# Gate and up products of a feed-forward layer: one level of block products in 22 units, or two levels in eleven quads

## The chip, the core and the metric

One Trainium2 chip, one core. The metric is device time in microseconds (us) of the whole kernel, median of three runs. A core has a matmul engine (TensorE, PE in the rows; PEld is its weight load), a vector engine (VectorE, DVE), an activation engine (ScalarE, ACT), a general engine (GpSimd, POOL) and SyncE (SP), which here only issues DMA transfers. Each engine works through its own list of instructions in order; between engines, semaphores are waited for.

## The reference, cut to what matters

Two transformer blocks, one after the other, over 1024 tokens of width 1024, all float32. The change is in the feed-forward layer of the first block (D_FF is 2816, three taps):

```python
hn = rms_norm(h, norm_ffn_g[i])
gate = causal_depthwise_conv(hn @ w_ffn_gate[i], ffn_conv_w[i])
h = h + (jax.nn.silu(gate) * (hn @ w_ffn_up[i])) @ w_ffn_down[i]
hn = rms_norm(h, norm_ple_g[i])
h = h + (p[i] @ w_ple_proj[i]) * jax.nn.sigmoid(hn @ w_ple_gate[i])
```

The causal convolution adds, for each hidden channel, the gate value of this token, of the token before and of the one before that, each times its own tap. The second block ends in a squared-ReLU layer of hidden width 4096 (`mlp_w1_2`, `mlp_w2_2`).

## The kernel before

Activations lie with channels on the 128 partitions and tokens along the row. T is 1024 tokens, HALF is 512, P is 128.

**Gate and up, before.** For each of 11 pairs g of 128-channel hidden tiles there are two units, ("gate", g) and ("up", g), each with a 1 MB piece of weights (1024 by 256). A unit is cut into 2 by 2 blocks (input rows, output tiles and token halves) and multiplied with Strassen's seven block products instead of eight. Every product is four matmuls of 128x128 weights on 512 columns (`strassen`, L1936); the trace counts each float32 matmul twice, so a unit is 56 records and all of them 1232. GpSimd makes five weight sums per unit (`sum_of_blocks`, L285), ScalarE copies three products out of PSUM (L2146, L2147, L2151, L2155), VectorE adds the others to them in SBUF (`into`, L2236, one operand in PSUM). After gate, VectorE makes the convolution over all 1024 tokens in three steps per tile (`conv`, L2272 to L2274); ScalarE applies SiLU (L2161); after up, VectorE multiplies (`mul`, L2279); GpSimd makes the four sums T3, T1, T2, T4 of hidden blocks that the down product needs (L2397 to L2402). Seven hidden pieces of 256 KB each are then stored to DRAM (`store_pair`, L2051), three tiles in turn being used for them. The order of the work is written out by hand, unit by unit.

**Quads.** The second block's first MLP product is already made in another way, by the class `Quads`. A quad is 512 output channels of 1024 inputs on 1024 tokens. It is cut into 2 by 2 blocks and multiplied in seven block products by the Winograd form of Strassen, called items (q, m1) and run in the order m1 = 1, 2, 6, 7, 5, 4, 3; each item is cut once more, into seven passes m of two matmuls of 128x128 weights on 256 columns (`product`, L3496), so 14 matmuls or 28 records. Items of quad 0 are plain: 8 matmuls on 512 columns, 16 records (`plain_product`, L3513). Of an item, ScalarE copies passes 1, 5, 6 and 4 (`copy`, names t1, t5, t2, c21, L3533) and VectorE adds pass 2, 3 and 7 to the first three (`add_block`, c11, c12, c22, L3541). TensorE's list mixes two items. In the slot of item n it runs

```python
PASSES = ((1, 0), (7, -1), (5, 0), (2, 0), (4, -1), (6, 0), (3, 0))
```

so passes 7 and 4 of item n - 1 come within item n's slot. Pass 4 of item n waits until VectorE has made c22 of item n. GpSimd makes for each item four weight sums of 256 columns (`level_sums`, L3579 to L3584), at most three items ahead, and for each quad four of 1024 columns, S1 (L3559), S2 (L3563), S3 (L3566) and S4 (L3571). S2 of quad q waits for the last pass of item (q - 1, 3). VectorE puts the items of a quad together with seven additions of 1024 columns (L4731 in the second block, with the four T sums).

**The down product** of both layers is `LastProduct` (L3767), 28 late items over the hidden pieces read back from DRAM. SyncE issues its loads in order behind the last `store_pair`; VectorE makes a weight sum (L3809) and the right-hand sums (L3833 to L3838), GpSimd the left-hand sums (L3790 to L3795).

## Time and profile before

| what | us |
|---|---|
| median of three runs (3221.6 to 3223.73) | 3222.9 |
| span of the profiled execution, first to last instruction | 3218.1 |
| gate and up products, 806.1 to 1341.1 | 535 |
| down product of the first block, 1341.3 to 1588.3 | 247 |
| second block's quads, 2481.9 to 2842.8 | 361 |
| granted TensorE clock, mean of the span | 0.989 |

The profiled execution's own time is listed as its span; what lies around the span is taken from the median, which is 4.8 us above it. TensorE's records are modelled and overlap: a 512-column record reads 0.59 us but the next starts 0.43 us later, so start-to-start distances are what counts. On the other engines the same holds on a small scale.

### The profile page before, as it was taken

The numbers are of one execution on the slowest core, as the hardware profiler recorded it, in microseconds if no ns is written. First come the engines' busy times: TensorE is split into PE (matmuls) and PEld (weight loads), VectorE is DVE, ScalarE is ACT, GpSimd is POOL, SyncE is SP. The second block draws the span as 40 slices with busy tenths as digits, with TensorE's granted clock in tenths as the row PEclk, the third lists the DMA queues.
The fourth block names the chain that finished last, engine by engine and source line by source line (L and its number), as shares of the span: only waits on it lengthen the run. The fifth ranks groups of instructions, "written<-read, shape, count | busy, mean of one in ns | idle before, by whom it ended". The sixth has DMA issues, their size and how long they took to land.

```text
span 3218.1 us, 32376 instructions
## 1 busy us (share of the span) xinstructions
PE 3120.3 (97%) x12306; PEld 1914.3 (59%) x12306; DVE 1809.7 (56%) x2558; ACT 773.7 (24%) x1302; POOL 1101.7 (34%) x855
## 2 busy tenths in 40 slices
PE   8997998999999999999999999999999999999997
PEld 3445564864444444588644554544554588888886
DVE  2386887742544434487634754753124655567877
ACT  3343334321111111000212333413212344410002
POOL 0010020003333333455610100152014698855655
PEclk9999999999999999999999999999999999999998
DMA  4220111241222122475312211102112233366652
GB/s 140 66 66 27 53 31 53 66 158 65 79 98 85 63 98 85 168 260 194 129 53 80 66 53 57 62 33 90 62 53 78 105 138 144 118 232 246 228 191 91
DMA packets 206121, 334.88 MB, mean 104 GB/s; under 512 B 10128, under 2 KB 123280, under 8 KB 205200
## 3 DMA queue, kind: packets, MB, share of 16 engines
q1 hardware_dynamic: 205968, 332.81, 29.8%
q8 instruction: 100, 1.64, 0.2%
q14 instruction: 53, 0.43, 0.0%
HBM read 268.55 MB, written 64.23 MB: 103 GB/s over the span
## 4 chain that ended last, share of the span: by engine, by line
PE 86%; DVE 8%; POOL 3%; ACT 2%; issue 1%; DMA 1%; DVEq 0%; POOLq 0%; SPq 0%; ACTq 0%
PE psum L1936 16%; PE psum L3767 15%; PE psum L181 10%; PE psum L3496 8%; PE psum L2555 8%; PE psum L407 7%; PE psum L1981 3%; PE psum L4334 3%; PE psum L563 1%; DVE arena L1380 1%; DVE arena L1378 1%; PE psum L3513 1%; PE psum L4311 1%; PE psum L4272 1%; PE psum L1987 1%
## 5 line engine op out<-in xcount | busy, mean ns | idle before, releaser
L3767 PE MATMUL psum<-arena 128*128 128x256 f32 x2660 | 579.4, 381 | 7.1 <-POOL arena L3793 7.1
L3767 PEld LDWEIGHTS psum<-arena 128*128 128x128 f32 x2660 | 506.7, 191 | 78.8 <-POOL arena L3793 8.6
L1936 PE MATMUL psum<-arena 128*128 128x512 f32 x1232 | 530.1, 592 | 1.9 <-DVE arena L2314 1.9
L1936 PEld LDWEIGHTS psum<-arena 128*128 128x128 f32 x1232 | 233.7, 190 | 296.6 <-issue 291.5
L407 PE MATMUL psum<-arena 128*128 128x512 f32 x768 | 337.9, 599 | 7.1 <-DVE arena L1236 4.9
L181 PE MATMUL psum<-arena 128*128 128x512 f32 x768 | 332.4, 592 | 1.5 <-ACT arena L4504 1.5
L2236 DVE TENSOR_TENSOR arena<-arena,psum 128x512 f32<-128x512 f32 x176 | 117.0, 686 | 296.3 <-PE psum L1936 154.7
L407 PEld LDWEIGHTS psum<-arena 128*128 128x128 f32 x768 | 146.2, 192 | 189.6 <-issue 185.0
L181 PEld LDWEIGHTS psum<-arena 128*128 128x128 f32 x768 | 145.8, 190 | 182.1 <-issue 180.6
L2555 PE MATMUL psum<-arena 128*128 128x512 f32 x576 | 251.7, 595 | 0.0
L3496 PE MATMUL psum<-arena 128*128 128x256 f32 x1080 | 244.6, 380 | 6.3 <-DVE arena L3541 5.6
L285 POOL TENSOR_TENSOR arena<-arena 128x512 f32<-128x512 f32 x130 | 162.9, 1287 | 187.5 <-DMA arena<-w_ffn_gate 174.6
L3496 PEld LDWEIGHTS psum<-arena 128*128 128x128 f32 x1080 | 204.1, 190 | 38.5 <-DVE arena L3541 6.6
L2555 PEld LDWEIGHTS psum<-arena 128*128 128x128 f32 x576 | 109.1, 191 | 136.6 <-issue 136.6
L4731 DVE TENSOR_TENSOR arena<-arena 128x1024 f32<-128x1024 f32 x88 | 141.0, 1603 | 12.9 <-ACT arena L3524 8.4
L3790 POOL TENSOR_TENSOR arena<-arena 128x512 f32<-128x512 f32 (+1 forms) x49 | 71.5, 1459 | 209.8 <-PE psum L3767 61.8
L4851 POOL TENSOR_TENSOR arena<-arena 128x512 f32<-128x512 f32 x75 | 98.5, 1313 | 102.5 <-DVE arena L4608 71.1
L3376 POOL TENSOR_TENSOR arena<-small_sb,consts_sb 128x512 f32<-128x512 f32 x16 | 16.2, 1041 | 325.4 <-PE psum L2633 170.6
L2365 POOL TENSOR_TENSOR arena<-arena 128x512 f32<-128x512 f32 x42 | 56.4, 1343 | 170.3 <-ACT arena L2120 169.4
L1981 PE MATMUL psum<-arena 128*128 128x512 f32 x256 | 112.5, 592 | 0.0
L4334 PE MATMUL psum<-arena 128*128 128x512 f32 x224 | 97.0, 593 | 0.9 <-DVEq L241 0.9
L2146 ACT ACTIVATE arena<-psum 128x512 f32<-128x512 f32 x22 | 13.1, 597 | 320.3 <-PE psum L1936 320.3
(552 smaller groups left out, 4374.2 us busy)
## 6 DMA issues: line engine op xcount, KB each, us to landing
arena<-w_in SPq DMA_DIRECT2D x42, 1024.0 KB, 5.2
arena<-mlp_w SPq DMA_DIRECT2D x72, 512.0 KB, 7.0
arena<-w_ffn_down SPq DMA_DIRECT2D x36, 512.0 KB, 7.3
arena<-mlp_w SPq DMA_DIRECT2D x8, 2048.0 KB, 8.6
mlp_hidden_T<-arena SPq DMA_DIRECT2D x32, 512.0 KB, 2.6
arena<-mlp_hidden_T SPq DMA_DIRECT2D x16, 1024.0 KB, 5.6
arena<-w_out SPq DMA_DIRECT2D x12, 1024.0 KB, 5.2
mlp_hidden_B<-arena SPq DMA_DIRECT2D x24, 512.0 KB, 2.6
```

What stands on the lines that cost most here:

```text
L181: mm = nc.tensor.matmul(self.out(i, x.shape[1]), part, x, start=(kk == 0), stop=(kk == self.kt - 1))
L285: return g.tensor_tensor(to[:, 0:kn, :], block_of(*a), block_of(*b), op)
L407: mm = nc.tensor.matmul(ps, slot(u)[:, k, m * P:(m + 1) * P], hn(k, h), start=(k == 0), stop=(k == KD - 1))
L1936: mm = nc.tensor.matmul(ps, left, right, start=(k == 0), stop=(k == 3))
L1981: mm = nc.tensor.matmul(ps, raw(v)[:, k, m * P:(m + 1) * P], half_of(env, N0, k, h), start=(k == 0), stop=(k == KD - 1))
L2236: return v_.tensor_tensor(dst, dst, tiles.ps(*key), op)
L2555: mm = nc.tensor.matmul(ps, slot(n)[:, k, m * P:(m + 1) * P], x_half(k, h), start=(k == 0), stop=(k == KD - 1))
L3496: mm = self.env.nc.tensor.matmul(self.ps(n, m), left[:, k, :], right[:, k, :], start=(m in (1, 5, 2) and k == 0), stop=(k == 1), skip_grou ...
L3767: mm = self.env.nc.tensor.matmul(ps[:, 256 * r:256 * r + 256], left[:, s, r * P:(r + 1) * P], right[:, s, :], start=(first and s == 0 and ...
L4334: mm = nc.tensor.matmul(ps, left, mix_right[m](k), start=(k == 0), stop=(k == 3))
L4731: blocks.mark(v_.tensor_tensor(to, one, two, op), name, q)
L4851: fin(pool, nc.gpsimd.tensor_tensor(dst, dst, src, ALU.add), sem, value)
```

## The change

Gate and up of a pair become one quad of 512 output channels: the left two tiles of it are gate, the right two are up. Eleven quads and 77 items take the place of 22 units; quad 0 is plain, ten quads run in two levels. The products' parts are put together by seven additions per quad (`combine`). The convolution is made per token half h: ScalarE makes the tap of this token with one Identity activation for each of the two tiles (`first_tap`), VectorE adds the other two (`conv`); for the second half two more pairs of instructions, of two and of one column, add what comes from the first half, whose last two columns were put aside (`past`). `mul` is per token half. The T sums go from GpSimd to VectorE. There is one hidden buffer instead of three, so the first tap of quad g waits until the pieces of quad g - 1 are stored. GpSimd now makes `level_sums`. Two thirds of the constants' tile is used as buffer meanwhile and read back from DRAM (one DMA of 128x1280 words). The down product's items and products are the same; its buffers lie elsewhere and its first loads are issued in another order. The second block is as before.

```diff
-            for unit in strassen_units[2:]:
-                for m in order_of[unit[0]]:
-                    strassen(unit, m)
+            for n, m in passes(LAST_N, quads.plain):
+                if m in ("p0", "p1"):
+                    quads.plain_product(pe, n, m)
+                else:
+                    quads.product(pe, n, m)
+                if (n, m) == (0, "p0"):
+                    sum_squares(1)
+                elif (n, m) == (0, "p1"):
+                    root_rows(1)
...
+    items = [(0, 1), (0, 2), (1, 1), (1, 2)] + [(0, m1) for m1 in QUAD_ORDER[2:]] + [(1, m1) for m1 in QUAD_ORDER[2:]]
+    items += [(q, m1) for q in PAIRS[2:] for m1 in QUAD_ORDER]
...
+            q, m1 = items[n]
+            added = [(name, q) for name in {6: ("U2", "C11"), 7: ("U3",), 5: ("U4", "C22"), 4: ("C21",), 3: ("C12",)}.get(m1, ())]
+            if q == 1 and m1 in (3, 6, 7, 5):
+                added += {6: ends(0)[1:2], 7: ends(0)[2:4], 5: ends(0)[4:], 3: ends(1)[1:2]}[m1]
+            elif m1 in (3, 4):
+                added += {3: ends(q)[0:1] if q == 0 else ends(q)[1:2], 4: ends(q)[0:1] if q else []}[m1]
+            elif m1 in (1, 2):
+                added += {1: ends(q - 1)[2:4], 2: ends(q - 1)[4:]}[m1]
...
+            def first_tap(g, h):
+                hidden.wait(act, ("C11", "C12")[h], g)
+                if h == 0:
+                    if g:
+                        act.wait_ge(*stored(g - 1))
+                    else:
+                        made_late.wait(act, at_item[0, 3], "p1")
+                        hidden.wait(act, "C12", 0)
+                for r in range(2):
+                    ins = nc.scalar.activation(hid(h)[:, r, :], (a_, c_)[h][g > 0][:, r, :], ACT.Identity, scale=tap(2, 2 * g + r))
+                copy.mark(ins, "tap", g, h)
...
-            def conv(g, j):
-                i, from_, to = 2 * g + j, made["gate"][j], hid(j, g)
-                if g >= 3 and j == 0:
-                    dve.wait_ge(*stored(g - 3))
-                step.step(dve, v_.tensor_scalar(to, from_, tap(2, i), None, ALU.mult))
-                step.step(dve, v_.scalar_tensor_tensor(to[:, 1:T], from_[:, 0:T - 1], tap(1, i), to[:, 1:T], ALU.mult, ALU.add))
-                hidden.mark(v_.scalar_tensor_tensor(to[:, 2:T], from_[:, 0:T - 2], tap(0, i), to[:, 2:T], ALU.mult, ALU.add), "conv", g, j)
+            def conv(g, h):
+                copy.wait(dve, "tap", g, h)
+                to, from_ = hid(h), (a_, c_)[h][g > 0]
+                taps = lambda j: [tap(j, 2 * g + r) for r in range(2)]
+                if h == 0:
+                    v_.tensor_copy(past, from_[:, :, HALF - 2:HALF])
+                base = step.n
+                for r in range(2):
+                    step.mark(v_.scalar_tensor_tensor(to[:, r, 1:], from_[:, r, 0:HALF - 1], taps(1)[r], to[:, r, 1:], ALU.mult, ALU.add))
+                for r in range(2):
+                    dve.wait_ge(tap_done, base + 1 + r)
+                    ins = v_.scalar_tensor_tensor(to[:, r, 2:], from_[:, r, 0:HALF - 2], taps(0)[r], to[:, r, 2:], ALU.mult, ALU.add)
+                if h:
+                    for r in range(2):
+                        step.mark(v_.scalar_tensor_tensor(to[:, r, 0:2], past[:, r, :], taps(0)[r], to[:, r, 0:2], ALU.mult, ALU.add))
+                    for r in range(2):
+                        dve.wait_ge(tap_done, base + 3 + r)
+                        ins = v_.scalar_tensor_tensor(to[:, r, 0:1], past[:, r, 1:2], taps(1)[r], to[:, r, 0:1], ALU.mult, ALU.add)
+                hidden.mark(ins, "conv", g, h)
...
+            def mul(g, h):
+                to = hid(h)
+                copy.wait(dve, "silu", g, h)
+                hidden.mark(v_.tensor_tensor(to, to, (d_, e_)[h][g > 0], ALU.mult), "mul", g, h)
...
+            for n in range(LAST_N + 1):
+                if two_level(n - 1):
+                    quads.add_block(dve, n - 1, "c22")
...
+                for key in added_after(n - 2)[1:]:
+                    add_up(key)
+                if two_level(n):
+                    quads.add_block(dve, n, "c11")
+                    if n == LAST_N - 1:
+                        late.right_sums(dve, 0)
+                    quads.add_block(dve, n, "c12")
+                for key in added_after(n - 1)[:1]:
+                    add_up(key)
...
+            conv(10, 1)
             late.right_sums(dve, 1)
+            for key in ends(10)[2:]:
+                add_up(key)
...
             store_pair(10)
             late.load_hidden(sp, 3, before_late_load)
+            sp.dma_start(env.consts[:, 2 * P:12 * P], dr["consts"][:, 2 * P:12 * P]).then_inc(w_summed, 16)
```

TensorE's list from the end of the mixers' output product on; `-` is before, `+` is the changed kernel. L1936 and L3651 work on 512 columns, L3634 is the quads' `product`; the counts are matmuls, two records each.

```order
-L1936 MATMUL psum<-arena 128x512 x4
 L292 MATMUL psum<-consts_sb,arena 128x1 x4
-L1936 MATMUL psum<-arena 128x512 x4
+L3651 MATMUL psum<-arena 128x512 x4
 L299 MATMUL psum<-consts_sb,arena 128x128 x4
-L1936 MATMUL psum<-arena 128x512 x608
-L3767 MATMUL psum<-arena 128x256 x508
+L3651 MATMUL psum<-arena 128x512 x8
+L3634 MATMUL psum<-arena 128x256 x26
```

616 matmuls on 512 columns become 56 of the plain quad and 980 on 256 columns.

VectorE's list before, from the second convolution tile of a pair to its first `mul`: L2236 is `into`, L2272 to L2274 the convolution, L2279 `mul`.

```order
L2272 TENSOR_SCALAR arena<-arena,cols_sb 128x1024 [waits taken1_0]
L2273 SCALAR_TENSOR_TENSOR arena<-arena,cols_sb 128x1023 [waits tap_done_1]
L2274 SCALAR_TENSOR_TENSOR arena<-arena,cols_sb 128x1022 [waits tap_done_1]
L2236 TENSOR_TENSOR arena<-arena,psum 128x512 [waits made_0,copied_1,taken2_0]
L2236 TENSOR_TENSOR arena<-arena,psum 128x512 [waits made_0,copied_1]
L2236 TENSOR_TENSOR arena<-arena,psum 128x512 [waits made_0]
L2236 TENSOR_TENSOR arena<-arena,psum 128x512
L2236 TENSOR_TENSOR arena<-arena,psum 128x512 [waits taken5_0,made_0]
L2236 TENSOR_TENSOR arena<-arena,psum 128x512
L2236 TENSOR_TENSOR arena<-arena,psum 128x512 [waits taken6_0,made_0]
L2279 TENSOR_TENSOR arena<-arena 128x1024 [waits copied_1,taken7_0]
```

The seven additions between the convolution and `mul` take products out of PSUM that TensorE has banks for; nothing on TensorE waits for `conv` or `mul` themselves.

VectorE's list in the changed kernel at the same place, the slots of items (q, 2) and (q, 6): the second token half's convolution (L2350 to L2359) of quad q - 1, then c11 (`conformer`), c12 (`consts_sb`), `mul` of the first half (L2365) and c22.

```order
L2350 SCALAR_TENSOR_TENSOR arena<-arena,cols_sb 128x511 [waits copied_1]
L2350 SCALAR_TENSOR_TENSOR arena<-arena,cols_sb 128x511
L2353 SCALAR_TENSOR_TENSOR arena<-arena,cols_sb 128x510 [waits tap_done_1] x2
L2356 SCALAR_TENSOR_TENSOR arena<-small_sb,cols_sb,arena 128x2 x2
L2359 SCALAR_TENSOR_TENSOR arena<-small_sb,cols_sb,arena 128x1 [waits tap_done_1] x2
L3679 TENSOR_TENSOR arena<-psum,conformer 128x256 [waits ones_made_0,copied_1,hid_ready_1]
L3679 TENSOR_TENSOR arena<-psum,consts_sb 128x256 [waits ones_made_0,copied_1]
L2365 TENSOR_TENSOR arena<-arena 128x2x512 [waits copied_1]
L3679 TENSOR_TENSOR arena<-psum,conformer 128x256 [waits ones_made_0,copied_1]
```

The convolution and the first `mul` stand ahead of c22, the last row, in one list.

SyncE's list in the changed kernel around the last store of hidden pieces (L2154), the load of late item 3's hidden piece and what follows; before, the row of L2190 is not there.

```order
L2154 DMA ffn_hidden_B<-arena 128x512 [waits hid_ready_1]
L2154 DMA ffn_hidden_B<-arena 128x512 x2
L2154 DMA ffn_hidden_T<-arena 128x512 x4
L3842 DMA arena<-ffn_hidden_B 128x2x512 [waits consts_in_0,mem_in_0,ones_made_0]
L2190 DMA consts_sb<-consts 128x1280
L3842 DMA arena<-ffn_hidden_T 128x2x1024 [waits cols_in_0,mem_in_0,consts_in_0,ones_made_0]
L3861 DMA arena<-w_ffn_down 128x2x512 [waits ones_made_0]
```

The loads of late item 4 still come behind the store, with one DMA more between.

## Rows read from the trace of the kernel before

**Rows 1.** The page: busy time of each engine over the span.
```profile
PE 3120.3 (97%) x12306; PEld 1914.3 (59%) x12306; DVE 1809.7 (56%) x2558; ACT 773.7 (24%) x1302; POOL 1101.7 (34%) x855
```

**Rows 2.** Timeline of TensorE: start, length (us), line, operation, count, [idle before].
```profile
806.09 3.60 PE L1936 MATMUL psum<-arena 128*128 128x512 f32 x8
...
815.57 1.16 PE L299 MATMUL psum<-consts_sb,arena 128*128 128x128 f32 x8 [1.55 <-DVE arena L2217]
```

**Rows 3.** Timeline of TensorE from the last unit to the down product.
```profile
1341.13 52.89 PE L3767 MATMUL psum<-arena 128*128 128x256 f32 x244
1395.30 5.02 PE L3767 MATMUL psum<-arena 128*128 128x256 f32 x22 [1.28 <-POOL arena L3793]
```

**Rows 4.** Chain of waits in order of time: start, length, what.
```profile
758.19 48.07 PE psum L181 x112
...
2481.87 3.43 PE psum L3513 x8
...
2842.77 290.27 PE psum L3767 x1344
```

**Rows 5.** Timeline of ScalarE, copies in the second block's quads: t2, t1, t5, t2.
```profile
2733.95 0.39 ACT L3533 ACTIVATE consts_sb<-psum 128x256 f32<-128x256 f32 x1 [0.48 <-PE psum L3496]
2735.67 0.39 ACT L3533 ACTIVATE conformer<-psum 128x256 f32<-128x256 f32 x1 [1.34 <-PE psum L3496]
2737.40 0.39 ACT L3533 ACTIVATE conformer<-psum 128x256 f32<-128x256 f32 x1 [1.34 <-PE psum L3496]
...
2739.99 0.38 ACT L3533 ACTIVATE small_sb<-psum 128x256 f32<-128x256 f32 x1 [0.48 <-PE psum L3496]
```

**Rows 6.** Groups of VectorE instructions by form: busy, mean ns, idle before.
```profile
L2273 DVE SCALAR_TENSOR_TENSOR arena<-arena,cols_sb 128x1023 f32<-128x1023 f32 x22 | 28.2, 1284 | 0.8
...
L2279 DVE TENSOR_TENSOR arena<-arena 128x1024 f32<-128x1024 f32 x20 | 24.5, 1225 | 0.7
...
L3541 DVE TENSOR_TENSOR arena<-psum,conformer 128x256 f32<-128x256 f32 x86 | 36.1, 420 | 20.4 <-PE psum L3496 19.7
```

**Rows 7.** Timeline of ScalarE: four instructions that scale 512 columns.
```profile
2502.91 2.55 ACT L4504 ACTIVATE arena<-arena,cols_sb 128x512 f32<-128x512 f32 x4
```

**Rows 8.** Timeline of GpSimd in the second block's quads: S2, s4, S3.
```profile
2715.00 2.36 POOL L3563 TENSOR_TENSOR arena<-arena 128x1024 f32<-128x1024 f32 x1 [2.69 <-PE psum L3496]
...
2720.47 0.73 POOL L3584 TENSOR_TENSOR arena<-arena 128x256 f32<-128x256 f32 x1
2721.16 2.36 POOL L3566 TENSOR_TENSOR arena<-arena 128x1024 f32<-128x1024 f32 x1
```

**Rows 9.** Timelines of VectorE and GpSimd: tiny additions beside GpSimd's.
```profile
196.64 1.20 DVE L1378 TENSOR_TENSOR arena<-arena 128x60 f32<-128x60 f32 x1
...
200.35 0.25 DVE L1380 TENSOR_TENSOR arena<-arena 128x87 f32<-128x87 f32 x1
...
195.26 4.96 POOL L1659 TENSOR_TENSOR arena<-arena,consts_sb 128x512 f32<-128x512 f32 x4 [6.09 <-DVE arena L1369]
```

**Rows 10.** The same: a multiply-add beside GpSimd's additions.
```profile
3050.89 3.24 DVE L4772 SCALAR_TENSOR_TENSOR arena<-arena 128x2048 f32<-128x2048 f32 x1
...
3051.95 3.31 POOL L3793 TENSOR_TENSOR arena<-arena 128x512 f32<-128x512 f32 x1
```

**Rows 11.** The same: 512 columns on VectorE against 256 on GpSimd.
```profile
2539.02 1.10 DVE L3596 TENSOR_TENSOR arena<-arena 128x512 f32<-128x512 f32 x1
...
2539.54 1.19 POOL L3580 TENSOR_TENSOR consts_sb<-arena 128x256 f32<-128x256 f32 x1
```

**Rows 12.** Busy us by stretch (PE, PEld, DVE, ACT, POOL), clock, DMA share, GB/s.
```profile
2640.00:2810.00 170.00, 169.97 (x784) 148.40 (x783) 97.15 (x128) 73.28 (x144) 150.35 (x129) 1.00 0.35 130
```

**Rows 13.** Start of the down product: DMAs issued by SyncE, and VectorE.
```profile
1350.15 3.13 SPq L2051 DMA_DIRECT2D ffn_hidden_T<-arena  x4
...
1358.10 2.73 SPq L3723 DMA_DIRECT2D arena<-w_ffn_down  x4
...
1369.52 2.29 DVE L3809 TENSOR_TENSOR arena<-arena 128x2048 f32<-128x2048 f32 x1 [6.72 <-DMA arena<-w_ffn_down]
```

More of the change, by code:

```diff
@@ L1832, in weights_of, with passed @@
             return down[:, q + 5 * c:q + 5 * c + n, j]
+        def passed(eng, m1):
+            made_late.wait(eng, *quads.last_pass(at_item[10, m1]))
         def before_late_bank(pe, at):
-            tiles.wait_free(pe, late_banks[at])
+            b = late_banks[at]
+            if at == 0:
+                tiles.wait_free(pe, b)
+                return
+            n, kind = max((n, m) for n in range(LAST_N - 3, LAST_N) for m in (1, 2, 3) if quads.bank_of(n, m) == b)
+            if kind == 1:
+                copy.wait(pe, "c21", n)
+            else:
+                hidden.wait(pe, {2: "c11", 3: "c12"}[kind], n)
```

605 lines of the change are left out of this document (333 added, 272 removed).

## The prediction, made before the changed kernel was run

> **What bounds the kernel now.** I read the page first: TensorE is busy 97% of the span, the next engine 56% [rows 1]. So the end is set by how many matmul columns there are and by what TensorE waits for; every other engine matters only where TensorE waits for it. The timeline of TensorE comes next. Gate and up run from 806.09 to 1341.13, 535.0 us, without a break but for a few waits in the first microseconds, of which the longest is 1.55 [rows 2, 3]. At the seam to the down product TensorE goes on at once and first waits 1.28 us at 1395.30 [rows 3]. Third, I read the second block's quads, since the changed kernel makes gate and up by the same code: the chain of waits has them from 2481.87 to 2842.77 [rows 4]. Last come the timelines of VectorE and GpSimd, to see how these two hold each other up.
>
> **TensorE's work.** The price of a 512-column record is the distance in a full stretch: 112 records in 48.07 us, 0.4292 each [rows 4]. Before: 1232 x 0.4292 = 528.8 us. The price of a two-level item is the distance of one and the same copy in two items that follow each other: 2739.99 - 2733.95 = 6.04 us [rows 5], which is 28 records of 0.2157. After: the plain quad has 7 x 16 = 112 records on 512 columns, 48.1 us; ten quads have 70 items of 6.04 us, 422.8. Together 470.9, which is 57.9 less. The two statistics matmul groups between the first products are in both. Of the 535.0 us, 528.8 are products and about 1.9 statistics, so 4.3 are waits of the start, which go: the reciprocal behind the 1.55 us wait no longer stands behind an addition on VectorE that needs a product. Term: -62.2.
>
> **Start of the quads.** The second block's quads take 360.9 us [rows 4], where 7 x 16 x 0.4292 + 49 x 6.04 = 344.0 and about 3.5 of statistics leave 13.4 of waits. Here the start has the same chain on GpSimd (three operands' sums, three quad sums and the item sums before the first two-level items of quad 1), but less is waited for at the very beginning, since the operand sums of the first block come before the scaling of the second half ends. On the other side, conv(0, 0) now stands before c22 of the second item of quad 1. I take 9, between 3 and 14.
>
> **One place in each quad.** From here on I count from the start of the slot of item (q, 2), called 0; the next slot, of item (q, 6), starts at 6.04. TensorE wants c22 of item (q, 2) for pass 4, the fifth pass of that next slot, 6.04 + 4 x 0.863 = 9.5. What VectorE must do before it, by its list: the second half's convolution of quad q - 1 (four multiply-adds of 511 or 510 columns, two of two and two of one column), c11, c12, mul of the first half, c22.
> It starts with the first tap on ScalarE. ScalarE copies t1 0.95 into the slot (one pass and 0.09), t5 1.73 later (2737.40 - 2735.67) for 0.39 [rows 5], so the tap starts at about 3.05; two scalings of 512 columns at 2.55 / 4 = 0.64 each, the last ending 0.1 later, give 4.4 [rows 7]. VectorE's convolution starts at 4.45.
> Undisturbed it takes 4 x 0.66 (half of 1.284 and a semaphore), 4 x 0.22 for the small ones (the 0.25 us row is the nearest [rows 9]) = 3.5, to 8.0; c11 and c12 0.34 each, mul 1.23, c22 0.42 [rows 6]: 10.35. TensorE waits 0.9 us.
> But GpSimd works beside it. Its S2 waits for the last pass of the quad before, 1.6 us before our slot, and S3 starts 6.16 later (2721.16 - 2715.00) and takes 2.36 [rows 8], which is 4.5 into the slot: just as the convolution starts. Item sums follow it without a gap. What that does can be seen elsewhere in the trace [rows 9]: beside four GpSimd additions of 1.24 us, a VectorE addition of 60 columns takes 1.20 (so do its neighbours, four in all, one for each of GpSimd's), and one of 87 columns falls back to 0.25 when GpSimd's are over. A multiply-add and an addition hold each other up alike [rows 10]. A pair, 512 columns against 256, takes about 1.15 [rows 11]. c22's kind, with one operand in PSUM, keeps its 420 ns beside GpSimd [rows 6]. With strict turns: first multiply-add to 5.05, S3 and the second to 8.0, two more pairs to 10.3, four small ones each behind an item sum of 0.69 (2721.16 - 2720.47 [rows 8]), to 13.1, c11 and c12 to 13.8, mul to 15.1, c22 to 15.5. TensorE waits 15.5 - 9.5 = 6.0 us.
> The Trainium skill, page "SBUF — State Buffer", section "SBUF: two separate sides", states that VectorE with two SBUF inputs and GpSimd share a port pair as an exclusive lock, held for the whole instruction. By that rule the 6.0 would hold in every quad, and the change would lose; the rows agree, and that case is the second rival.
> I take 5.4: in the second block's quads GpSimd is busy 150.35 of 170 us, 88% [rows 12], so 0.9 + 0.88 x 5.1. The place comes in the slots (q, 2) for q = 2 to 10, nine times: +48.6, with bounds of 8 (0.9 each) and 63 (7 each, S2 or another long sum in the way too). Below 0.9 there is nothing, as no list gets shorter by the wait.
> Costed at nothing: ScalarE's work (28 copies, 4 taps and 2 SiLU in a quad are about 15 us of 42); the wait of the first tap for the stores of the quad before (the T sums end some 24 us into our count, their stores 8 later as before [rows 13], the tap comes at 36); conv of the first half, which falls where GpSimd waits for S2; quad weight loads, 2 MB in 42 us. If the cover of the stores were gone, that would cost a few us per quad.
>
> **Seam to the down product.** VectorE ends quad 10 with conv(10, 0), C12, the tap, conv(10, 1), a right sum, two mul and four T sums: 3 + 1.2 + 1.4 + 3.5 + 0.4 + 2.5 + 2.6 = 14.6 us after TensorE's last pass, and the stores of the T pieces start 1.4 behind the last sum, at 16. Before, they started at 1350.15, 9 us after TensorE's last unit, and the loads behind them at 1358.10 [rows 13], 17 us after. Now these loads come at about 24, and 1 more for the constants' DMA. The weights then landed for the sum at 1369.52 [rows 13], 11.4 later, just in time (1.28 us wait [rows 3]). So late item 3 waits about 1.5, item 4 (needed at 33.7, after 156 records of 0.2157; its sum ready at 25 + 11.4 + 2.3 = 38.7) about 5, and 1.5 more for GpSimd's sums, less the 1.28. I take +7, between 3 and 11. The last c22 adds 0.5.
>
> **Sum.** -62.2 + 9 + 48.6 + 0.5 + 7 = +2.9. The profiled span 3218.1 becomes 3221.0; the median of the runs lies 4.8 above the span, so 3225.8, call it 3226. A measurement of this kernel can tell about 0.2%, 6.4 us, from no change.
>
> **Rivals.** First, the turns rarely meet: GpSimd is done or waits for its ring when the convolution comes, or takes its turns between. For it speaks that GpSimd stands idle 20 of 170 us there [rows 12] and VectorE is busy for 57% only; against it, that S3 falls on the spot. Each place costs 1 to 3.5 us: -62.2 + 7 + 9 x 2.2 + 0.5 + 6 = -29, 3194. It decides from 4.4 us per place down, where the sum passes -6.
> Second, and on the other side, c22 in full turns everywhere: 6.0 to 7 us per place, and a quad costs as much as two units did (42.3 + 6 against 112 x 0.4292 = 48.1), so that only the plain quad and the start are left as gain, and seam and start take them: -62.2 + 12 + 9 x 6.6 + 0.5 + 8 = +18, 3241. It decides from 5.8 us per place up.
> Third, GpSimd or another list becomes the bound over the whole quad, not at one place: VectorE's work on two SBUF operands is 9 x 1.23 + 12 x 0.66 = 19 us in a quad and GpSimd's alone 28 x 0.69 + 4 x 2.4 = 29, together more than the 42.3; a steady wait spread over many items would give 45 to 50 us a quad and anything from 3200 to 3260. For it speaks the 88%; against it, that GpSimd in the second block still waits 2.69 us for TensorE before an S2 [rows 8]. That the change would not do what it says can be excluded from TensorE's list.
>
> **How the numbers follow.** My forecast (each place 4.4 to 5.8) has 0.40, the first rival 0.30, the second 0.20, the third 0.10. Faster by over 0.2%: the first rival, a few hundredths of the third, 0.05 of the forecast's lower end, 0.37. Slower: the second, most of the third, the forecast's upper end, 0.36. Within 0.2%: 0.27. The forecast alone, with the start and the seam, spans 3213 to 3235; the range for 8 in 10 reaches into both rivals, from 3190 (1.8 us per place) to 3246.
>
> **What will show it.** In the timeline of TensorE: 28 records per 6.04 us between the waits, 1960 + 112 records in all, and in each quad one idle stretch of about 5 us before pass 4 in the slot of item (q, 6), put down to VectorE's add_block, L3679. In VectorE's timeline L2350 to L2359 stretched from 0.67 and 0.2 to about 1.15 (one near 3) and 0.7. If these stand at 0.67 and 0.2, the first rival holds. If TensorE's waits are spread over items and name GpSimd's level sums, the third. The prediction is wrong in its main step if the idle stretches name another list: the stores, ScalarE's copies or the loads. At the seam, the first weight sum of the down product should start about 7 us later, counted from TensorE's last quad pass, than it did (28.4).

## The result, and the profile after

| | before | after |
|---|---|---|
| median of the runs, us | 3222.25 (4 runs) | 3280.36 (3277.49 to 3281.84, 4 runs) |
| profiled span, us | 3218.1 | 3278.4 |
| gate and up, from TensorE's first product to its last pass | 535.0 | 583.7 |
| down product, to the next statistics | 247.0 | 254.9 |
| second block's quads | 360.9 | 363.3 |

The ratio is 1.018, with a 95% interval of 1.0165 to 1.0194: 58 us slower, where 3226 us and at most 3246 were forecast. The first line of the page, which answers to [rows 1]: TensorE is busy for less time than before, and the time is longer.

```profile
PE 3098.1 (95%) x13146; PEld 2088.2 (64%) x13146; DVE 2024.9 (62%) x2806; ACT 864.7 (26%) x1552; POOL 1293.7 (39%) x1025
```

Where the time goes shows in one quad of TensorE's timeline (start, length, line, shapes, count, [idle before]; L3634 is the quads' product). The rows left out are passes without a wait.

```profile
1185.16 1.89 PE L3634 MATMUL psum<-arena 128*128 128x256 f32 x8
1188.73 6.31 PE L3634 MATMUL psum<-arena 128*128 128x256 f32 x28 [1.68 <-DVE arena L3679]
1200.11 7.40 PE L3634 MATMUL psum<-arena 128*128 128x256 f32 x20 [5.08 <-DVE arena L3679]
...
1215.51 0.70 PE L3634 MATMUL psum<-arena 128*128 128x256 f32 x2 [0.23 <-DVE arena L3679]
```

Two things to see. Every quad has three waits for VectorE's additions (L3679), not one: 1.68 for c22 of item (q, 1), 5.08 for c22 of (q, 2), 0.23 later on. And the 20 records behind the 5.08 us take 7.40 us, where 20 records behind a wait of 1.70 us, one quad later, take 4.58:

```profile
1241.90 4.58 PE L3634 MATMUL psum<-arena 128*128 128x256 f32 x20 [1.70 <-DVE arena L3679]
```

The busy times by stretch say why (us of PE, PEld, DVE, ACT, POOL, then the granted clock of TensorE, DMA share, GB/s):

```profile
1189.00:1195.00 6.00, 6.00 (x28) 4.96 (x27) 5.26 (x4) 2.19 (x5) 5.84 (x5) 1.00 0.00 0
...
1200.10:1204.00 3.90, 3.89 (x9) 3.17 (x10) 1.43 (x2) 0.45 (x2) 0.00 (x0) 0.50 0.02 4
1204.00:1208.00 4.00, 4.00 (x16) 3.29 (x16) 1.40 (x4) 0.70 (x2) 0.41 (x1) 0.77 0.00 0
1208.00:1215.00 7.00, 7.00 (x34) 6.08 (x32) 6.50 (x7) 1.92 (x5) 6.84 (x6) 1.00 0.44 162
```

Before the wait the clock is 1.00 (2.4 GHz), behind it 0.50 (1.2 GHz) for the first 4 us, and 0.77 on the mean of the next 4. From one 1.68 wait to that of seven quads later are 366.3 us (979.35 to 1345.69), 52.3 a quad; 42.3 is its work.

VectorE's timeline up to that wait, the place the prediction worked out:

```profile
1188.26 0.41 DVE L3679 TENSOR_TENSOR arena<-psum,conformer 128x256 f32<-128x256 f32 x1
1189.74 3.21 DVE L2350 SCALAR_TENSOR_TENSOR arena<-arena,cols_sb 128x511 f32<-128x511 f32 x2 [1.07 <-ACT arena L2253]
1192.87 2.35 DVE L2353 SCALAR_TENSOR_TENSOR arena<-arena,cols_sb 128x510 f32<-128x510 f32 x2
1195.14 1.35 DVE L2356 SCALAR_TENSOR_TENSOR arena<-small_sb,cols_sb,arena 128x2 f32<-128x2 f32 x2
1196.42 1.44 DVE L2359 SCALAR_TENSOR_TENSOR arena<-small_sb,cols_sb,arena 128x1 f32<-128x1 f32 x2
...
1198.44 1.28 DVE L2365 TENSOR_TENSOR arena<-arena 128x1024 f32<-128x1024 f32 x1
1199.65 0.41 DVE L3679 TENSOR_TENSOR arena<-psum,conformer 128x256 f32<-128x256 f32 x1
```

The eight multiply-adds take 8.1 us, and a multiply-add of one or two columns takes 0.7. At the end of the last quad, where GpSimd stands idle, the same two small pairs take 0.34 us each:

```profile
1397.65 0.34 DVE L2356 SCALAR_TENSOR_TENSOR arena<-small_sb,cols_sb,arena 128x2 f32<-128x2 f32 x2
1397.91 0.34 DVE L2359 SCALAR_TENSOR_TENSOR arena<-small_sb,cols_sb,arena 128x1 f32<-128x1 f32 x2
```

The wait that wasn't foreseen, 1.68, begins eight microseconds earlier. Timelines of VectorE and GpSimd there:

```profile
1177.75 2.60 DVE L2389 TENSOR_TENSOR arena<-arena 128x1024 f32<-128x1024 f32 x1
...
1182.00 3.98 DVE L2353 SCALAR_TENSOR_TENSOR arena<-arena,cols_sb 128x510 f32<-128x510 f32 x2
...
1176.91 2.36 POOL L3697 TENSOR_TENSOR arena<-arena 128x1024 f32<-128x1024 f32 x1
1181.95 2.35 POOL L3701 TENSOR_TENSOR arena<-arena 128x1024 f32<-128x1024 f32 x1 [2.69 <-PE psum L3634]
```

GpSimd's S1 (L3697) ends at 1179.27, and VectorE's C21 (L2389), which takes 1.2 us elsewhere, is stretched to 2.60 by it. So the first half's convolution begins 1.4 us into the 2.69 us that GpSimd waits before S2 (L3701). Its first pair of multiply-adds fits into the rest, its second pair meets S2 and takes 3.98. So c22 of (q, 1) is late.

### The profile page after: what moved, and what is told of

Its sections match the earlier page's. It is cut to its first block, busy times and chain, and to the rows that moved or that the text cites. A ratio compares the mean times of both kernels' runs of the same rounds, so it can differ in the third digit from the quotient of the medians.

```text
span 3278.4 us, 35350 instructions
## 1 busy us (share of the span) xinstructions
PE 3098.1 (95%) x13146; PEld 2088.2 (64%) x13146; DVE 2024.9 (62%) x2806; ACT 864.7 (26%) x1552; POOL 1293.7 (39%) x1025
## 3 DMA queue, kind: packets, MB, share of 16 engines
q8 instruction: 108, 1.77, 0.2%
## 4 chain that ended last, share of the span: by engine, by line
PE 78%; DVE 13%; issue 3%; POOL 2%; ACT 2%; DMA 1%; SPq 0%; DVEq 0%; POOLq 0%; ACTq 0%
PE psum L3634 17%; PE psum L3905 15%; PE psum L181 10%; PE psum L2690 8%; PE psum L407 7%; PE psum L2083 3%; PE psum L4472 3%; PE psum L3651 3%; DVE arena L2350 1%; PE psum L563 1%; DVE arena L1380 1%; DVE arena L1378 1%; DVE arena L2389 1%; DVE arena L2353 1%; DVE arena L3679 1%
## 5 line engine op out<-in xcount | busy, mean ns | idle before, releaser
L3634 PE MATMUL psum<-arena 128*128 128x256 f32 x2632 | 621.0, 390 | 81.7 <-DVE arena L3679 76.8
L3634 PEld LDWEIGHTS psum<-arena 128*128 128x128 f32 x2632 | 510.7, 195 | 171.4 <-DVE arena L3679 85.9
L3905 PE MATMUL psum<-arena 128*128 128x256 f32 x2660 | 582.4, 382 | 11.5 <-POOL arena L3931 6.4
L3905 PEld LDWEIGHTS psum<-arena 128*128 128x128 f32 x2660 | 508.2, 191 | 84.3 <-POOL arena L3931 7.6
L407 PE MATMUL psum<-arena 128*128 128x512 f32 x768 | 338.2, 599 | 7.2 <-DVE arena L1236 4.9
L181 PE MATMUL psum<-arena 128*128 128x512 f32 x768 | 332.4, 592 | 1.5 <-ACT arena L4642 1.5
L407 PEld LDWEIGHTS psum<-arena 128*128 128x128 f32 x768 | 146.3, 192 | 189.8 <-issue 185.0
L181 PEld LDWEIGHTS psum<-arena 128*128 128x128 f32 x768 | 145.8, 190 | 182.1 <-issue 180.6
L2690 PE MATMUL psum<-arena 128*128 128x512 f32 x576 | 250.9, 594 | 0.0
L2690 PEld LDWEIGHTS psum<-arena 128*128 128x128 f32 x576 | 108.8, 190 | 136.0 <-issue 136.0
L3634 PE MATMUL psum<-arena,consts_sb 128*128 128x256 f32 x632 | 157.9, 384 | 3.8 <-POOL consts_sb L3717 3.3
L3671 ACT ACTIVATE conformer<-psum 128x256 f32<-128x256 f32 x238 | 89.8, 382 | 251.0 <-PE psum L3634 249.9
L4869 DVE TENSOR_TENSOR arena<-arena 128x1024 f32<-128x1024 f32 x88 | 145.6, 1655 | 12.9 <-ACT arena L3662 7.9
L2389 DVE TENSOR_TENSOR arena<-arena 128x1024 f32<-128x1024 f32 x77 | 133.1, 1729 | 9.8 <-ACT arena L3662 9.8
L4989 POOL TENSOR_TENSOR arena<-arena 128x512 f32<-128x512 f32 x75 | 98.5, 1313 | 102.4 <-DVE arena L4746 70.9
L3634 PEld LDWEIGHTS psum<-arena,consts_sb 128*128 128x128 f32 x632 | 121.9, 193 | 22.0 <-POOL consts_sb L3717 3.7
L3679 DVE TENSOR_TENSOR arena<-psum,conformer 128x256 f32<-128x256 f32 x238 | 99.4, 418 | 56.1 <-PE psum L3634 52.7
L2528 POOL TENSOR_TENSOR arena<-arena 128x512 f32<-128x512 f32 x42 | 57.2, 1361 | 181.0 <-ACT arena L2224 180.1
L3717 POOL TENSOR_TENSOR arena<-arena 128x256 f32<-128x256 f32 x79 | 79.9, 1011 | 89.2 <-PE psum L3634 86.4
L2083 PE MATMUL psum<-arena 128*128 128x512 f32 x256 | 112.5, 592 | 0.0
```

The source lines that it names most:

```text
L181: mm = nc.tensor.matmul(self.out(i, x.shape[1]), part, x, start=(kk == 0), stop=(kk == self.kt - 1))
L407: mm = nc.tensor.matmul(ps, slot(u)[:, k, m * P:(m + 1) * P], hn(k, h), start=(k == 0), stop=(k == KD - 1))
L2083: mm = nc.tensor.matmul(ps, plain_raw(v)[:, k, m * P:(m + 1) * P], half_of(env, N0, k, h), start=(k == 0), stop=(k == KD - 1))
L2389: hidden.mark(v_.tensor_tensor(to, one, two, ALU.add), name, q)
L2690: mm = nc.tensor.matmul(ps, slot(n)[:, k, m * P:(m + 1) * P], x_half(k, h), start=(k == 0), stop=(k == KD - 1))
L3634: mm = self.env.nc.tensor.matmul(self.ps(n, m), left[:, k, :], right[:, k, :], start=(m in (1, 5, 2) and k == 0), stop=(k == 1), skip_grou ...
```

## The experiments

All against the kernel before, and each run starts from the changed kernel. "A quad" is the mean distance between equal places of the steady quads in TensorE's timeline.

### 1. GpSimd quiet

```diff
+        cut = (lambda ap: ap[:, 0:1, 0:1]) if self.first and n >= 14 else (lambda ap: ap)
+        p11, p12, p21, p22 = [cut(p) for p in (p11, p12, p21, p22)]
```

> From the third quad on, GpSimd makes the four item sums of every item (L3717 to L3722) on a single column instead of 256, so the products of these items are wrong from there; the quad's own four sums S1 to S4 stay whole. Nothing moves on any list. Theory (turns): in the changed kernel the two full multiply-adds of a row of the second half and its two small ones take 2 x 3.98/2 and 2 x 1.4/2 us because each waits for an instruction of GpSimd; with GpSimd quiet the four large ones take 0.70 each and the small ones 0.17 (the durations at the seam, where GpSimd is idle), the block in front of c22 of item (q,2) falls from 10 us to about 6, TensorE's wait of 5.1 us a quad falls under 1.5, the 20 slow passes behind it go, and a quad takes 42.3 to 44 us in place of 52.5: 3195 to 3215 us. Rival (the order alone: VectorE has too much in front of c22, GpSimd or not): the wait stays at 4 us or more and the kernel at 3262 to 3280. Second rival (ScalarE's taps come late): multiply-adds get short, but VectorE idles in front of them, and the time stays over 3250.

GpSimd's four sums of an item are cut to one column here, from quad 2 on; its sums S1 to S4 stay. Measured: 3202.53 us, 0.9939 of before (0.9924 to 0.9953). Groups of VectorE's instructions by form (busy us, mean ns, idle before), first of the changed kernel, then of this run, from 1031 to 1345 in both:

```profile
L2353 DVE SCALAR_TENSOR_TENSOR arena<-arena,cols_sb 128x510 f32<-128x510 f32 x24 | 38.0, 1620 | 0.0
...
L2359 DVE SCALAR_TENSOR_TENSOR arena<-small_sb,cols_sb,arena 128x1 f32<-128x1 f32 x12 | 8.6, 756 | 0.0
```

```profile
L2354 DVE SCALAR_TENSOR_TENSOR arena<-arena,cols_sb 128x510 f32<-128x510 f32 x28 | 19.6, 742 | 0.0
...
L2360 DVE SCALAR_TENSOR_TENSOR arena<-small_sb,cols_sb,arena 128x1 f32<-128x1 f32 x14 | 2.4, 208 | 0.0
```

And its timeline of TensorE, where one wait stands for a quad:

```profile
1194.09 1.13 PE L3636 MATMUL psum<-arena 128*128 128x256 f32 x4 [0.89 <-DVE arena L3681]
```

Nothing on VectorE's list was moved, yet a one-column multiply-add falls from 756 to 208 ns, and the wait that is left is 0.89 us: the undisturbed price of 0.9 in the prediction. A quad takes 43.5 us (1150.63 to 1194.09). The wait for c22 of (q, 1) is gone too. The C21 that S1 had stretched and the second pair that had met S2 are short again:

```profile
1178.11 1.22 DVE L2390 TENSOR_TENSOR arena<-arena 128x1024 f32<-128x1024 f32 x1
...
1181.23 1.41 DVE L2354 SCALAR_TENSOR_TENSOR arena<-arena,cols_sb 128x510 f32<-128x510 f32 x2
```

S1 is over at 1177.37 in this run, before C21 begins, and S2 starts at 1182.06, when the convolution has 0.6 us to go. The rival "order alone" falls, and so does the one about ScalarE's taps, since VectorE still idles for them (1.71 us before the convolution at 1187.97) and the time is gained all the same.

### 2. Work in the wait, too much of it

```diff
         elif m == 4:
+            if self.first is not None and m1 == 2 and 2 <= q <= 10:
+                b = self.first
+                for k in range(20):
+                    self.env.nc.tensor.matmul(self.env.ps(b * BANK, b * BANK + BANK // 2), self.left(n, 4)[:, k % 2, :],
+                                              self.right(n, 4)[:, k % 2, :], start=(k == 0), stop=(k == 19), skip_group_check=True)
             self.blocks.wait(pe, "c22", n)
```

> In quads 2 to 10 TensorE does 20 further matmuls of 256 columns into the PSUM bank that nobody uses there, right before the pass for which it waits 5.1 us for c22 of item (q,2); their result is not used. 20 x 0.216 = 4.3 us of work, all inside the wait. Theory (clock): the 20 passes after the wait take 7.40 us instead of 4.32 because the engine stood idle and the granted clock fell to 0.50; with work in the wait the clock stays at 1.00, they take 4.32, and a quad gets 3.1 us shorter although it has more work: 9 x 3.1 = 28, so 3252 us (3246 to 3258). Rival (the passes are slow for another reason: operands, memory, a pipeline that fills): they stay at 7.4 us and the kernel at 3277 to 3285. If the wait is shorter than the work in some quads, each such quad gives back what stands over.

Measured: 3296.63 us, 1.0233 of before (1.0218 to 1.0248), above every band I had given. The size was a slip of mine: a matmul is two records, so the added work was 8.6 us, longer than the wait. The clock can be read all the same. TensorE's rows (L3634 is the added work), and the stretch behind it:

```profile
1152.50 8.80 PE L3634 MATMUL psum<-arena 128*128 128x256 f32 x40
1161.13 10.52 PE L3641 MATMUL psum<-arena 128*128 128x256 f32 x48
```

```profile
1161.10:1171.50 10.40, 10.40 (x50) 9.13 (x50) 6.30 (x9) 2.69 (x7) 5.73 (x5) 1.00 0.14 51
```

48 records in 10.5 us at a clock of 1.00, and no slow ones.

### 3. Work in the wait, the right size

The same with `range(10)`.

> The busy wait again with 10 matmuls in place of 20 in quads 2 to 10. The profile counts two records for a matmul of 256 columns, so the 20 of the run before were 40 records and 8.64 us, more than the wait of 5.1 us; 10 matmuls are 20 records and 4.32 us, and fit. Theory (clock): a rest of the wait of about 0.8 us stays, the 20 passes behind it run at full clock (4.32 us, not 7.40), and nine quads each get 2.4 to 3.1 us shorter: 3250 to 3259 us. Rival (the idle time itself is all that was lost, and the slow passes come from elsewhere): they stay at 7.40 us and the kernel at 3275 to 3282.

Measured: 3265.53 us, 1.0132 of before (1.0117 to 1.0147), 14.8 below the changed kernel, with 90 further matmuls in it. Its timeline of TensorE, and the stretch behind the wait:

```profile
1140.95 4.48 PE L3634 MATMUL psum<-arena 128*128 128x256 f32 x20
1146.17 10.63 PE L3641 MATMUL psum<-arena 128*128 128x256 f32 x48 [0.74 <-DVE arena L3686]
```

```profile
1146.10:1150.50 4.40, 4.33 (x20) 3.84 (x21) 2.50 (x5) 1.15 (x3) 0.00 (x0) 1.00 0.00 0
```

4.3 us of work and 0.74 of wait take the place of 5.07 of wait, so nothing else changed, and a quad falls from 52.3 to 50.35 us (983.70 to 1336.17, seven quads). That the slow clock comes from the idle engine is shown. My size was off: I had read 3.1 us from one quad. The 56 records from this wait to the next one take 12.35 us here in every quad; in the changed kernel they take 13.74 to 15.36, so 1.4 to 3.0 us are lost in a quad, on the mean 2.1. The time missed the band I had given by 6.5 us.

### 4. Without the small multiply-adds

```diff
-                if h:
+                if h and g in (0, 10):
```

> For gate quads 1 to 9 the four multiply-adds on two columns and on one (L2356, L2359) of the second half are left out, so two columns of the hidden states are wrong. Theory (turns): beside GpSimd each takes 0.65 to 0.75 us, so 2.8 us a quad go from the block in front of c22 of item (q,2); TensorE's wait falls from 5.1 to about 2.3 us, and of the 3.1 us of slow clock a part or all goes with it: 3226 to 3256 us. Rival (the size of the work counts: 0.17 us each with GpSimd idle, 0.7 together): 3270 to 3276.

Measured: 3249.32 us (3248.15 to 3261.07), 1.0089 of before (1.007 to 1.0108), 31 below the changed kernel, for 36 instructions on one or two columns. TensorE's wait goes to 2.9 us, and behind it the clock mostly holds and sometimes does not:

```profile
1131.76 12.31 PE L3634 MATMUL psum<-arena 128*128 128x256 f32 x48 [2.90 <-DVE arena L3679]
...
1181.59 4.58 PE L3634 MATMUL psum<-arena 128*128 128x256 f32 x20 [2.89 <-DVE arena L3679]
```

48 records take 10.63 in experiment 3, here 12.31. Of the eight waits of 2.9 us in quads 3 to 10, two were followed by such a loss of 1.7 us. A quad takes 48.4 us: 2.2 less of wait and about 1.7 less of slow clock.

### 5. The first tap on VectorE again

```diff
+                for r in range(2):
+                    step.mark(v_.tensor_scalar(to[:, r, :], from_[:, r, :], taps(2)[r], None, ALU.mult))
```

> One part of the change undone: the first tap is made by VectorE again, one multiply by a column for each row, and ScalarE's two taps shrink to one column each (kept for their signals). All else is as in the changed kernel. If the tap on ScalarE is a gain as counted: VectorE gets four more instructions of 0.35 to 0.7 us a quad and loses its wait of 1.07 us for ScalarE, so the block in front of c22 of (q,2) changes by -0.4 to +0.4 us and that in front of c22 of (q,1) by +0.7 to +1.4: 3281 to 3300 us. Rival (the way through ScalarE is what makes the block late): 3265 to 3277.

Measured: 3295.97 us, 1.0224 of before (1.0207 to 1.0241), 15.6 above the changed kernel. So this part of the change is a gain. The wait for c22 of (q, 2) got shorter in seven quads of nine (of the 1.07 us for ScalarE 0.21 are left), that of (q, 1) longer in all, and now the clock mostly falls behind both:

```profile
1193.12 8.00 PE L3637 MATMUL psum<-arena 128*128 128x256 f32 x28 [3.03 <-DVE arena L3682]
1205.01 7.28 PE L3637 MATMUL psum<-arena 128*128 128x256 f32 x20 [3.89 <-DVE arena L3682]
```

28 records take 6.31 us behind the 1.68 of the changed kernel, 8.00 here.

### 6. The convolution by rows, spread over the items

For gate quads 1 to 9, what VectorE does before c11 and after c12 of each item:

```diff
+            return {1: [("conv", q - 1, 0, 1)], 2: [("C12", q - 1)], 6: [("conv", q - 1, 1, 1)], 7: [("mul", q - 1, 1)],
+                    5: [("T3", q - 1), ("T1", q - 1), ("T2", q - 1), ("T4", q - 1)], 4: [("U3", q)], 3: [("C22", q)]}[m1]
...
+            return {1: [("C21", q - 1)] * (q > 2), 2: [("conv", q - 1, 1, 0)], 6: [("mul", q - 1, 0)], 7: [("U2", q)], 5: [("C11", q)],
+                    4: [("U4", q)]}[m1]
```

> Same work; for gate quads 1 to 9 the convolution is cut by rows (two of a half each) and spread: a half's two rows stand in two different items, and in no item do more than about 3.5 us of sums stand between one c22 and the next; the taps and the activation follow. Theory (a block too long in front of c22, made so by turns): no c22 is late any more, TensorE's waits of 7.0 us a quad fall under 1.5, and with them the slow clock: 43 to 45 us a quad, so 3198 to 3222. Rival (VectorE and GpSimd together are the limit: 39.2 and 36.3 us busy of 52.5, more than 42.3 us hold once both run at once): the waits only spread, a quad takes 47 to 51 us, 3235 to 3270.

Measured: 3230.15 us, 1.0024 of before (1.0013 to 1.0034). A quad takes 46.2 us (1033.03 to 1310.25, six quads): no slow clock is left in these quads, and waits of 1.76, 0.48 and 0.36 us come again in each. That lies between the theory and the rival. The waits of TensorE from 800 to 1345 (total, times, longest) have one thing that neither had:

```profile
PE psum L3678 <- DVE arena L3723: 35.1, 32, 5.7
PE psum L3678 <- ACT small_sb L3715: 11.7, 1, 11.7
```

The 11.7 us come once, where ScalarE's first tap of quad 1 waits for the stores of quad 0 and t2 stands behind it. Without them the time would lie in the theory's band (3218).

### 7. The rows in the spare PSUM bank

```diff
+    spare = env.ps(at_bank(2) * BANK, (at_bank(2) + 1) * BANK)
...
+                    copy.mark(nc.scalar.activation(spare, (a_, c_)[h][g > 0][:, r, :], ACT.Identity, scale=tap(2, 2 * g + r)), *((name,) + key))
...
+                copy.mark(nc.scalar.activation(hid(h)[:, r, :], spare, ACT.Silu), *((name,) + key))
...
+                to, from_ = spare, (a_, c_)[h][g > 0]
...
+                step.step(dve, v_.scalar_tensor_tensor(to[:, 1:], from_[:, r, 0:HALF - 1], tap_of(1), to[:, 1:], ALU.mult, ALU.add))
+                ins = v_.scalar_tensor_tensor(to[:, 2:], from_[:, r, 0:HALF - 2], tap_of(0), to[:, 2:], ALU.mult, ALU.add)
```

> As the run with the rows spread, and besides ScalarE writes the first tap of one row into the spare PSUM bank, VectorE adds the two other taps there, and ScalarE's activation reads the bank and writes the row of the hidden states: a multiply-add then has one operand in SBUF and one in PSUM. Theory: such instructions take no turns (as L3679, 0.42 us beside GpSimd and without it): 0.7 us each and 0.2 for the small ones, VectorE's busy time falls from 39 to about 33 us a quad, and the kernel is at 3195 to 3212, below the run with the spread rows by up to 15 us. Rival (turns cost the same with PSUM, or ScalarE's chain of tap, activation, tap now sets the pace): multiply-adds stay over 1 us, or VectorE idles in front of them, and the time is that of the other run or above it.

Measured: 3205.67 us, 0.9951 of before (0.9934 to 0.9968); GpSimd is as busy as ever. VectorE's groups, first of experiment 6, then of this run:

```profile
L2399 DVE SCALAR_TENSOR_TENSOR arena<-arena,cols_sb 128x511 f32<-128x511 f32 x25 | 26.0, 1042 | 1.7 <-ACT arena L2285 1.7
...
L2403 DVE SCALAR_TENSOR_TENSOR arena<-small_sb,cols_sb,arena 128x1 f32<-128x1 f32 x14 | 9.1, 646 | 0.5
```

```profile
L2415 DVE SCALAR_TENSOR_TENSOR psum<-arena,cols_sb,psum 128x511 f32<-128x511 f32 x24 | 18.0, 750 | 16.8 <-ACT psum L2304 16.8
...
L2419 DVE SCALAR_TENSOR_TENSOR psum<-small_sb,cols_sb,psum 128x1 f32<-128x1 f32 x12 | 2.7, 224 | 0.4
...
L2414 DVE COPY small_sb<-arena 128x4 f32<-128x4 f32 x6 | 9.3, 1548 | 0.0
```

750 and 224 ns beside a busy GpSimd are what the same instructions take in SBUF with GpSimd quiet (742 to 890 and 208 in experiment 1). A quad takes 44.3 us (1038.60 to 1215.67). The four-column copy of the first half's last columns, now at another place, takes 1548 ns: a tiny copy pays too.

### 8. Quad 0 in the same way, the copy on ScalarE

```diff
+                return {9: [("C12", 0), ("conv", 0, 0, 1)], 10: [("U2", 1), ("conv", 0, 1, 0)], 11: [("U3", 1), ("conv", 0, 1, 1)],
+                        12: [("U4", 1), ("mul", 0, 1)], 13: [("C22", 1), ("conv", 1, 0, 0)]}[n]
...
+                    if (h, r) == (0, 0):
+                        nc.scalar.activation(past, a_[g > 0][:, :, HALF - 2:HALF], ACT.Copy)
```

> The run with rows in the spare PSUM bank, with quad 0 (whose sums fall into the second quad) cut and spread in the same way, and the copy of the last two columns of the first half (1.55 us on VectorE beside GpSimd in that run, 0.15 without) moved to ScalarE. Theory: of the three waits at the start of the products (3.3, 4.4 and 4.1 us) and the 7 us of slow clock behind them most goes, since the same kind of block stands in front of those c22: 3187 to 3200 us. Rival (they wait for the sums of the operands and for the products themselves): 3202 to 3208, as the run before.

Measured: 3192.55 us, 0.9905 of before (0.989 to 0.992): the fastest kernel of this study, 31 us below before and 88 below the changed kernel. Of the waits of the start none is above 2.06 us, slow records follow only that one (four in 2.05 us, where four take 1.10 behind the others), and a quad takes 43.65 us with one wait:

```profile
1115.67 10.63 PE L3701 MATMUL psum<-arena 128*128 128x256 f32 x48 [1.08 <-DVE arena L3746]
...
1159.36 4.58 PE L3701 MATMUL psum<-arena 128*128 128x256 f32 x20 [1.11 <-DVE arena L3746]
```

### 9. The constants later

```diff
-            sp.dma_start(env.consts[:, 2 * P:12 * P], dr["consts"][:, 2 * P:12 * P]).then_inc(w_summed, 16)
...
                 late.load_weights(sp, n, before_late_load)
+                if n == 10:
+                    sp.dma_start(env.consts[:, 2 * P:12 * P], dr["consts"][:, 2 * P:12 * P]).then_inc(w_summed, 16)
```

> The changed kernel with one transfer moved: the reload of the constants (L2190, 640 KB) is issued after the weights of item 10 of the down product instead of between the last loads of hidden states and the weights of item 4. At the seam VectorE waits 9 us for those weights, TensorE then 4.2 us for VectorE's sum of them (L3947), and the DMA engines are full there at 380 GB/s. Theory (the seam's 8 us are a queue of transfers): 640 KB at 380 GB/s are 1.7 us, so the weight sum starts 1.7 us earlier, TensorE's wait falls from 4.2 to about 2.5 us and the slow clock behind it with it: 3275 to 3279 us, to be read in the trace more than in the time. Rival (the weights wait for TensorE to free their places, or for the T sums): nothing moves, 3280.

Measured: 3279.88 us, 1.018 of before (1.0166 to 1.0194), which can't be told from the changed kernel. The trace can. TensorE at the seam in the changed kernel, then in this run, whose last quad pass comes 1.1 us later:

```profile
1429.77 6.04 PE L3905 MATMUL psum<-arena 128*128 128x256 f32 x16 [4.16 <-issue]
1436.04 9.30 PE L3905 MATMUL psum<-arena 128*128 128x256 f32 x42 [0.22 <-DVE arena L4002]
```

```profile
1428.79 3.69 PE L3906 MATMUL psum<-arena 128*128 128x256 f32 x16 [2.10 <-issue]
1435.05 25.29 PE L3906 MATMUL psum<-arena 128*128 128x256 f32 x109 [2.57 <-DVE arena L4003]
```

The wait falls by 2.1 and the 16 records behind it by 2.35, since the clock is 1.00 there (0.60 in the changed kernel); 2.35 of that is given back at the next row, where TensorE is early enough to wait for VectorE. So TensorE is 2.1 us ahead at this place. Not all of it stays: the clock now falls behind the 2.57 us instead (0.61 over the next 4 us, 1.00 at this place in the changed kernel), and the whole down product takes 254.2 us for 254.9.

### 10. The T sums dealt out

In the kernel of experiment 8, with the constants later:

```diff
-                    5: [("T3", q - 1), ("T1", q - 1), ("T2", q - 1), ("T4", q - 1)], 4: [("U3", q)], 3: [("C22", q)]}[m1]
+                    5: [("T1", q - 1), ("T2", q - 1)], 4: [("T4", q - 1), ("U3", q)], 3: [("C22", q)]}[m1]
```

> The run with all quads cut into rows in the spare bank, with two moves: the four T sums of a quad (4 x 1.4 us beside GpSimd, one block in front of c22 of item (q,5), for which TensorE waits 1.1 us in each quad) are dealt over three items, and the reload of the constants stands later, as in the other run of this call. Theory: no block in front of a c22 is longer than the slot leaves, the 1.1 us go in nine quads, and the seam gains 1.7 us: 3178 to 3186 us. Rival (the block only moves: U2, T3 or U3 now stands in front of another c22 by as much): 3190 to 3196.

Measured: 3196.94 us, 0.9921 of before (0.9907 to 0.9935), by its median 4.4 above experiment 8, so no gain. My theory falls, and what the rival says holds, with a time just above its band. The block is now U2 and T3:

```profile
1152.42 2.84 DVE L2446 TENSOR_TENSOR arena<-arena 128x512 f32<-128x512 f32 x1
...
1155.65 10.63 PE L3702 MATMUL psum<-arena 128*128 128x256 f32 x48 [1.35 <-DVE arena L3747]
...
1309.32 2.07 PE L3702 MATMUL psum<-small_sb,arena 128*128 128x256 f32 x4 [5.57 <-DVE arena L3747]
...
1304.84 0.69 DVE L4039 TENSOR_TENSOR arena<-arena 128x512 f32<-128x512 f32 x1 [3.20 <-DMA arena<-ffn_hidden_B]
```

T3 alone (the first row) takes 2.84 us where it stands now, the wait is 1.35 in place of 1.08, and the last quad has a wait of 5.57 that experiment 8 has as 2.20. The last row shows where this one comes from: in front of the last c12 and c22 VectorE's list has the first right-hand sums of the down product (L4039), and these wait 3.20 us for a hidden piece to be loaded. SyncE issues that load behind the stores of quad 9, which begin at 1295.23 here and at 1287.60 in experiment 8, where the sums start without a wait.

## Why the prediction was wrong

Gate and up took 52.8 us more than the 530.9 of its terms, and that is nearly all of the miss. TensorE waited 78.8 us in this stretch (58.1 forecast) and worked 505.0 (472.8 forecast). The median missed 3226 by 54.4 us only, because the prediction put 4.8 us between span and median, where 2.0 lie now. By the steps of the prediction:

- **One place in each quad** was right in place, count and price: nine waits for c22 of (q, 2), 5.57 and eight of 5.05 to 5.08, together 46.1 where 48.6 were forecast. The cause was right too: with GpSimd quiet the eight multiply-adds take 3.9 us from first start to last end (8.1 in the changed kernel) and the wait is 0.89 (0.9 forecast), and with one operand in PSUM they are as short beside a busy GpSimd. The lock rule that the prediction quoted from the Trainium skill (page "SBUF — State Buffer", section "SBUF: two separate sides") gave 6.0 for this wait; the trace agrees with it in kind, since a one-column instruction pays 0.7 us, and the wait came out 0.9 lower.
- **"Conv of the first half, which falls where GpSimd waits for S2"** was the step that failed among the waits. I costed it at nothing. GpSimd does wait 2.69 us there, but S1 holds up VectorE's C21 before it, so that only half of the convolution falls into that wait and the other half meets S2: c22 of (q, 1) is late by 1.68 us eight times, 13.4 us. Nine waits of 0.23 add 2.
- **TensorE's work** was priced at full clock throughout, from stretches of before in which TensorE never stood still for long. That is the step that cost most. Behind each 5 us wait the clock was 0.50 to 0.65 over the next 4 us. Against the same number of records without a slow clock (12.35 us for 56) the stretch behind the 5.69 loses 2.8 us and those behind the nine waits for c22 of (q, 2) 18.6, together 21.4; experiment 3 gives 2.0 us a quad of it back by work alone. The other 10.8 of the 32.2 are no slow clock. Behind every wait the records take about 0.27 us more than the pace of [rows 5], also at a clock of 1.00 (28 records 6.31 us for 6.04). With 32 waits that is some 8.6 us, and small breaks in the passes add about as much again once a quad, 2.4.
- **Start of the quads**: 15.7 us of waits (3.27, 1.19, 5.69, 2.55 and 2.98) where 9 were taken, just beyond my bound of 14, and part of the slow clock besides. Experiment 8, with quad 0's sums cut and spread, waits 6.6 us up to the same place, so most of it was the same kind of block in front of a c22.
- **Last c22**: 1.49 for 0.5. **Seam**: +7.9 for +7, with the first weight sum 36.6 us after the last quad pass (28.4 before), 8.2 later where 7 were forecast (VectorE's four T sums alone took 5.72 us there, where 2.6 were counted). Experiment 9 shows that the constants' transfer has 2.1 us of this sum's delay in it, of which 0.7 are left at the end of the down product.
- The rest of the program, which the prediction left alone, is 2.8 us longer, 2.4 of it in the second block's quads. Their list is as before, and in both kernels TensorE waits 3.29 us at the same place. Behind it the clock was 1.00 before and 0.65 in the changed kernel (over 4 us), which costs 1.7 of the 2.4. No step of the change is known to cause that.

The sum of these: -2.5 + 13.4 + 2.0 + 21.4 + 10.8 + 6.7 + 1.0 = 52.8 for gate and up, +1 for a later start, 0.9 for the seam, 2.8 for the rest, 57.5 in all, against the 57.4 by which the span missed 3221.0.

Of the rivals, the second had the right side and a third of the size, but not its price: the place cost 5.1 us of wait and not 6.0 to 7, and what it lacked were the slow clock and the place before it. The third, a bound over the whole quad, is not what the changed kernel shows, since its waits stand at three places and name VectorE's `add_block`. Experiment 8 makes the same sums in 43.65 us a quad, though GpSimd is busy for 128.74 of 149 us there:

```profile
1031.00:1180.00 149.00, 145.73 (x674) 127.32 (x673) 106.17 (x155) 53.88 (x129) 128.74 (x108) 1.00 0.28 95
```

But its multiply-adds no longer have two SBUF operands. With both in SBUF and the work spread (experiment 3) a quad still takes 46.2 us, within the 45 to 50 of this rival. Whether another order could bring that to 43 was not tried. And the first, that the turns rarely meet, is refuted by the durations.

The change itself has a gain in it: the same products, with the convolution placed and fed otherwise (experiment 8), take 498.5 us for gate and up, where 535.0 were needed before, and the kernel is 1% faster than before.

## What to carry to other kernels

Price a wait of TensorE twice: its length, and the slower work behind it, read from the granted clock after waits of that length. Where VectorE has two SBUF operands beside a busy GpSimd, count its instructions and not their columns, and give it an operand in PSUM if a bank is free. When one block is found in front of a critical instruction, go through the same sum for each neighbour: the block I had costed at nothing was the next in the list.
